# Another order of the first products of the odd projection, and 20 TensorE passes of 256 columns that nothing reads, in the first attention

## The reference

```python
# first block, layer 0: "even" attention (differential and sparse heads), norm, MLP
h = x @ w_in_even
mix = concatenate([diff_attention(...), nsa_attention(...)]) @ w_out_even
x = layer_norm(ALPHA * x + mix)
x = layer_norm(ALPHA * x + square(relu(x @ w_up)) @ w_down)
# layer 1: "odd" attention
h = x @ w_in_odd                      # 1024 x (3 * 1024 + 16)
q, k, v, fl = split(h)                # fl: 16 forget logits a token
mix = forgetting_attention(q, k, v, fl) @ w_out_odd
...
# second block: windowed attention with context, 64 experts of which each token takes 8, final norm
```

## Time and profile before

| | |
|---|---|
| median of 3 runs | 1353.12 us |
| the runs | 1361.75, 1348.17, 1353.12 us |
| the profiled execution's own time | 1348.86 us |
| its span, first to last instruction | 1347.2 us |
| mean granted TensorE clock | 0.998 of 2.4 GHz |
| TensorE busy | 1317.1 us, 98% of the span |

### The profile page before, as it was taken

How to read it: one execution, slowest core, us unless ns; L and a number is a source line. 1 busy time by engine, 2 the same in 40 slices (tenths; PEclk the granted TensorE clock), 3 DMA queues, 4 the chain that set the end, 5 groups by cost and what they waited for, 6 DMA issues and landing times.

```text
span 1347.2 us, 19389 instructions
## 1 busy us (share of the span) xinstructions
PE 1317.1 (98%) x7490; PEld 818.7 (61%) x7490; DVE 679.6 (50%) x1260; ACT 234.1 (17%) x547; POOL 96.1 (7%) x116
## 2 busy tenths in 40 slices
PE   9999999999999999999999999999999999999996
PEld 8676585786679557587686666644444444444433
DVE  1226588877889549977878253421222122212213
ACT  2136211110120341120122252100000000000002
POOL 1116400000011120000000100000000000000001
PEclk9999999999999999999999999999999999999999
DMA  9921155554414535567664504499999999999994
GB/s 379 359 110 66 63 219 206 216 229 191 188 63 169 219 147 217 216 253 285 240 237 158 186 31 190 176 421 422 420 420 414 421 422 420 422 421 422 420 420 196
DMA packets 51008, 359.56 MB, mean 267 GB/s; under 512 B 5888, under 2 KB 6096, under 8 KB 8432
## 3 DMA queue, kind: packets, MB, share of 16 engines
q1 hardware_dynamic: 45248, 324.60, 59.7%
q0 software_dynamic: 5392, 32.05, 6.5%
q10 hardware_dynamic: 288, 1.80, 0.3%
HBM read 356.88 MB, written 1.05 MB: 266 GB/s over the span
## 4 chain that ended last, share of the span: by engine, by line
PE 76%; DVE 11%; DMA 2%; issue 2%; ACT 1%; DVEq 0%; SPq 0%; ACTq 0%
PE ps L1519 13%; PE ps L997 11%; PE ps L988 7%; PE ps L1548 7%; PE ps L1444 7%; PE ps L1497 7%; PE ps L970 5%; PE ps L1274 4%; DVE ring L2358 2%; PE ps L1269 2%; DVE masked_and_probs L2317 2%; DMA ring<-in_stream 2%; PE ps L890 1%; PE ps L909 1%; PE ps L851 1%
## 5 line engine op out<-in xcount | busy, mean ns | idle before, releaser
L2807 DVE TENSOR_TENSOR masked_and_probs<-ps,gate_rows 128x512 f32<-128x512 f32 x52 | 33.5, 686 | 152.4 <-PE ps L1548 152.4
L1497 PE MATMUL ps<-masked_and_probs,probT 128*128 128x512 f32 x208 | 94.4, 594 | 1.0 <-DVE masked_and_probs L2807 1.0
L1444 PE MATMUL ps<-masked_and_probs,mix_rows 128*128 128x256 f32 (+1 forms) x416 | 93.0, 376 | 0.0
L1444 PEld LDWEIGHTS ps<-masked_and_probs,mix_rows 128*128 128x128 f32 x416 | 75.0, 190 | 28.8 <-issue 19.6
L988 PEld LDWEIGHTS ps<-xT,ring 128*128 128x128 f32 x768 | 87.8, 192 | 3.8 <-issue 3.8
L988 PE MATMUL ps<-xT,ring 128*128 128x128 f32 x768 | 88.7, 275 | 0.0
L997 PE MATMUL ps<-ring,qk_tiles 128*128 128x512 f32 x192 | 85.2, 592 | 0.0
L970 PE MATMUL ps<-ring,xT 128*128 128x512 f32 x192 | 83.8, 593 | 0.0
L2795 DVE TENSOR_TENSOR masked_and_probs<-masked_and_probs,ps 128x256 f32<-128x256 f32 x26 | 10.9, 421 | 142.0 <-ACT masked_and_probs L1980 142.0
L1656 ACT ACTIVATE qk_tiles<-ps 128x512 f32<-128x512 f32 (+7 forms) x58 | 30.1, 521 | 244.4 <-PE ps L988 236.7
L1519 PE MATMUL ps<-ring,vec_rows 128*32 128x512 f32 (+2 forms) x296 | 72.0, 592 | 0.0
(11 more groups left out here) (498 smaller groups left out, 2368.1 us busy)
## 6 DMA issues: line engine op xcount, KB each, us to landing
ring<-in_stream SPq DMA_DIRECT2D x200, 1024.0 KB, 10.0
qk_tiles<-in_stream SPq DMA_DIRECT2D x46, 1024.0 KB, 20.3
v_rows<-in_ada POOLq DMA_DIRECT2D x12, 1024.0 KB, 5.2
qk_tiles<-in_ada POOLq DMA_DIRECT2D x12, 1024.0 KB, 5.1
vec_rows<-in_stream SPq DMA_DIRECT2D x12, 1024.0 KB, 17.7
con<-in_stream SPq DMA_DIRECT2D x12, 1024.0 KB, 18.6
y_rows<-in_stream SPq DMA_DIRECT2D x12, 1024.0 KB, 20.3
par<-in_stream SPq DMA_DIRECT2D x12, 1024.0 KB, 20.5
```

The source lines that it names most:

```text
L1444: mm = pe.matmul(ps[:, 5 + kk // 2, kk % 2 * 2 * P:kk % 2 * 2 * P + width], h2[:, t, k * P:(k + 1) * P], select[:, t, 0:width], start=t == ...
L1497: mm = pe.matmul(ps[:, q, :], probT[:, buf, 256 + q // 2 * P:256 + (q // 2 + 1) * P], yslot[:, q % 2 * 512:(q % 2 + 1) * 512], start=False ...
L2807: dve.tensor_tensor(yslot[:, cols], ps[:, 5 + half, :], gaterow[:, 1, cols], ALU.mult).then_inc(ready, 1)
```

## The change

In turns 14 to 33 of the first attention, TensorE does one more matmul of 256 columns (the identity against the cosine table, two passes), just ahead of the turn's transposes and into the bank that they then overwrite. It stands behind the wait for the copy of turn u - 2 and ahead of the wait for the turn's exponential; to allow that, the two waits change places in all turns.

At the start of the odd projection, the forget logits are made in two halves, the first of them directly behind `odd(0, 1)`; the transposes of the second half of the tokens move from ahead of `odd(0, 2)` into its middle; and ScalarE copies product 1 out before it copies the turned half 1.

```diff
+FILLED = {**dict.fromkeys(range(14, 34), 256)}
...
                     if a <= u < b:
                         nk = UNITS[u][3]
+                        if u >= 2:
+                            wait_probs(u - 2)
+                        if u in FILLED:
+                            pe.matmul(ps[:, 2 + u % 2, 0:FILLED[u]], ident, C("cos1")[:, 0:FILLED[u]], start=True, stop=True)
                         pe.wait_ge(s_exp, u + 1)
-                        if u >= 2:
-
-                            wait_probs(u - 2)
...
-            def few_columns(name, width, bank):
+            def few_columns(name, width, bank, cols=slice(0, T)):
...
-                    mm = pe.matmul(ps[lo:lo + 32, bank, 0:T], par[:, at + k * width:at + k * width + 32], xT[:, k, :],
+                    mm = pe.matmul(ps[lo:lo + 32, bank, cols], par[:, at + k * width:at + k * width + 32], xT[:, k, cols],
...
-            def odd(b, n, ks=range(4)):
+            def odd(b, n, ks=range(4), within=None):
...
                     for m in range(4):
+                        if within and m == 2:
+                            within()
...
             odd(0, 1)
-            turn_rows(x, "ln1", 1)
-            odd(0, 2)
+            few_columns("wforget", 16, 4, slice(0, P))
+            odd(0, 2, within=lambda: turn_rows(x, "ln1", 1))
             wait_columns("ln1", 1)
-            few_columns("wforget", 16, 4).then_inc(s_fcol, 1)
+            few_columns("wforget", 16, 4, slice(P, T)).then_inc(s_fcol, 1)
             odd(0, 3)
...
             mlp(0)
-            stds_and_turns("ln1")
+            std(0)
+            take_turn("ln1", xT, only=0)
+            std(1)
+            act.wait_ge(s_prod, odd_product(0, 1))
+            copy(odd_p1, ps[:, ODD_BANKS[0][1], :], scale=SCALE).then_inc(s_taken, 1)
+            take_turn("ln1", xT, only=1)
```

More of the change, by code:

```diff
@@ L902, in attention @@
                         nk = UNITS[u][3]
-                        pe.wait_ge(s_exp, u + 1)
                         if u >= 2:
                             wait_probs(u - 2)
+                        if u in FILLED:
+                            pe.matmul(ps[:, 2 + u % 2, 0:FILLED[u]], ident, C("cos1")[:, 0:FILLED[u]], start=True, stop=True)
+                        pe.wait_ge(s_exp, u + 1)
                         for t in range((nk + P - 1) // P):
@@ L1870, in _ @@
                 scale = SCALE if b == 0 else 1.0
-                act.wait_ge(s_prod, odd_product(b, 1))
-                copy(odd_p1, ps[:, ODD_BANKS[b][1], :], scale=scale).then_inc(s_taken, 1)
-                if b == 0:
+                if b:
+                    act.wait_ge(s_prod, odd_product(b, 1))
+                    copy(odd_p1, ps[:, ODD_BANKS[b][1], :]).then_inc(s_taken, 1)
+                else:
                     act.wait_ge(s_fcol, 1)
```

## The result

| | before | after |
|---|---|---|
| median of 12 runs beside each other | 1351.66 us | 1362.8 us |
| lowest and highest | 1347.38, 1361.75 us | 1351.73, 1368.05 us |
| profiled execution: own time, span | 1348.86, 1347.2 us | 1365.31, 1363.6 us |
| its mean granted clock | 0.998 | 0.985 |

The ratio is 1.0068 [1.0039, 1.0098]: slower, by the medians 11.1 us, by the means 8.6 us (1361.5 for 1352.9). The forecast was 1353.7 us, with a range of 1350 to 1360. Five of the twelve runs lie in that range and two near the forecast (1352.58 and 1355.19 us); six lie at 1365 to 1368 us and draw the median up.

A forecast was written before the change was run, and what follows sets the result against it. TensorE, busy for 98% of the span, was taken to bound the kernel. To the profiled 1348.86 us, 6.1 us for the passes were added and 1.3 us for the new order subtracted: 1353.7 us, range 1350 to 1360.

The forecast's parts named there:

- The price of the passes: First attention, turns 14 to 33: twenty matmuls cost 8.65 us of TensorE, of which 6.1 us are added.
- The hidden part: First attention: 2.3 to 2.7 us of the passes, taken as 2.55, fall where TensorE would have waited anyway.
- that rival (1350.6 us): First attention: VectorE hides most fillers, only those of turns 27 to 33 pay, 3.0 us; chance 0.12.
- The new order: Odd projection's start: product 3 begins 1.3 us earlier, with some 0.5 us of new waiting for VectorE; bounds 0 and 2.1.
- The rival by which it gives nothing: Odd projection: VectorE, moved back 1.2 us, is late for a later product, giving 1355.0 us; chance 0.08.
- The rest moves along: Behind the first attention: TensorE stays busy and loads move with it, so nothing of the shift is absorbed.
- The sum: Whole kernel: profiled execution's 1348.86 us + 6.1 - 1.3 = 1353.7 us; chance 0.5, own range 1352 to 1356.
- the one on the clock: At both edits: granted clock is 1.00, so there is none to give back and unread passes are pure cost.
- the slower draws have another cause and stay: Whole kernel: slow runs remain, so the middle of the runs carries the sum, 1353.12 + 4.8 = 1357.9 us; chance 0.2.
- the first rival: First attention: fillers hold a clock some executions lose, all runs at 1353.7 us; gain over 1% had chance 0.04.
- no idle time of TensorE there is longer than 1.4 us: Windows of both edits: short idle times, given beside the granted clock of 1.00, 2.4 GHz.
- The slower case: First attention's stretch: clock falls despite the passes; slower by over 1% from 13 us at lower level, 1366.7 us; chance 0.05.

The follow-up runs named there:

- c4: The changed kernel plus four 256-column matmuls that nothing reads in the second attention's wait for VectorE; median 1353.07 us, ratio to before 0.998.
- d4: Kernel before plus the 20 passes and four unread matmuls in the second attention's wait, old order of the odd projection; median 1355.26 us, ratio 1.0014.
- f4: Kernel before plus the 20 passes alone, old order of the odd projection, run a second time; median 1360.36 us, ratio 1.0042.
- c1: The control: kernel before with nothing changed, run for the clock of each run; median 1354.54 us, ratio 0.9997.
- d2: Changed kernel without the 20 passes, plus four unread matmuls in the second attention's wait; median 1349.45 us, ratio to before 0.9988.
- e2: Kernel before plus five unread 256-column matmuls in the first MLP's last step, everything behind 2.2 us later; median 1356.35 us, ratio 1.0025.
- e3: Kernel before plus eight unread 256-column matmuls in the first MLP's last step, everything behind 3.5 us later; median 1351.51 us, ratio 1.0001.
- f2: Changed kernel without the 20 passes, plus two unread matmuls in the first MLP's last step, 0.87 us of delay; median 1358.96 us, ratio to before 1.0011.
- c2: Kernel before plus the 20 passes alone, old order of the odd projection; median 1359.99 us, ratio 1.0024.
- d1: The changed kernel unchanged, run again beside the kernel before; median 1360.36 us, ratio to before 1.0071.
- c3: Kernel before plus the new order of the odd projection alone, no added passes; median 1355.48 us, ratio 1.0001.
- e1: Kernel before plus three unread 256-column matmuls in the first MLP's last step, everything behind 1.3 us later; median 1354.04 us, ratio 1.0003.

## Why the prediction was wrong

**The price of the passes: right.** Predicted 6.1 us added; 6.0 in the profile, 5.2 to 6.3 in the runs. The hidden part (2.55 us) was right with it, and VectorE did not hide more: that rival (1350.6 us) fell.

**The new order: right in mechanism and place, somewhat small.** Predicted 1.3 us with VectorE late ahead of product 3 by 0.5; the profile has 1.34 and 0.67. By the medians of c4 and d4 it is 2.2 us, and the split of the order alone gives 2.2 and 2.4. Where the other 0.9 us come from is not shown. The two profiles of c4 and d4 have 1.10 us, so it isn't at the edit; a short fall at the odd projection's start that the old order has in some runs (in f4's profile product 2 takes 5.4 us for the 3.8 of full clock) and the second layer's MLP, whose length varies by as much, are candidates. The rival by which it gives nothing fell.

**The rest moves along: nearly.** "I let nothing be absorbed" held to within 2.2 us: that much came back in the second layer's MLP in the profile of after, and 1.1 us in that of c4_gap_filled (5.35 us behind before at the second attention, 4.2 by the spans).

**The sum: right for the work.** 4.8 us predicted; 4.6 and 5.0 measured by the split, and 4.3 in c4_gap_filled, of which 0.7 are its filler. The forecast's 1353.7 us is within 0.6 us of c4_gap_filled's median, 1353.07, and within 1.3 of it less the filler.

**The step that failed is the one on the clock**: "In this execution there is no clock to give back, and passes that nothing reads are pure cost", and what was built on it: the likeliest case summed onto the profiled execution, near the lower edge of before's own runs, with "The clock reads 1.00 as before" as what the profile after would show. Of the 9.1 us between forecast and median, 2.8 are the base (before's median was 1351.66 us in the comparison, the profiled execution 1348.86) and nearly all the rest, some 6 us, is that after lost the clock more than before did. The term of the clock in the sum was nothing. The spread of before, 1348 to 1362 us, was seen and matched in size with a clock at half speed, but the places looked at were those of the edits. The runs showed three places where the clock falls in some executions: the first attention (profiles of c1, d2, e2, e3, f2), the start of the odd projection in the old order (c2, e2, f4) and, longest, the second attention behind a wait of 1.4 us (after, d1, c2, c3, e1, e2). The change seems to close the first two: in the first attention no profile of 8 with passes lost the clock, for 5 of 10 without; at the odd projection none of 10 with the new order, for 3 of 8 with the old, few enough to be chance. It leaves the third, the dearest: 6 of 13 profiles fall there, none of the 5 in which the wait is filled. Whether after's runs lost more there than before's is not shown, since no run tells where its clock fell; by the mean clock they lost more in all. So the rival "the slower draws have another cause and stay" (0.2, 1357.9 us) came nearest in mechanism, since the middle of the runs carries the sum; it lacked that the draws can also get worse, and its time was 4.9 us short of the median. Of the first rival, that the fillers hold a clock which some executions lose, one half held: they hold it where they stand. Its other half, that all runs then agree at 1353.7 us, needed one filler more, in a place of which the trace had the row: the 1.38 us wait at 461.03 us, as long as the one that the new order removes.

That "no idle time of TensorE there is longer than 1.4 us" was used as a reason for a full clock; just such waits precede the falls in two of the three places.

**The slower case** (the clock falls although the passes are there, from 13 us of work at the lower level, 0.05) happened in size in the profiled execution, but elsewhere: 34.1 us at the lower level cost 14.3 us, within its price of a half for each us spent there, in a stretch it didn't name.

By the Trainium skill's page "TensorE: Matmul & The Clock Gate" (Part 1, HAM oscillation) the clock falls to half after TensorE has waited. The direction was borne out in the second attention. The page's example is a wait on DMA of some 3 to 5 us, longer than any at the three places here, whose longest is 1.47 us (c3_order_only); TensorE was busy for four fifths of the 7 us ahead of the fall, and for nine tenths of the 3.4 us ahead in the control's first attention. The same page has it that transposes don't count as busy like matmuls (Part 4, PE-mode transpose). That would fit the first attention, but no run here isolates it.

## What to carry to other kernels

When the runs of a kernel spread by more than the edit is worth, take the mean clock of each run before anything else, and look for the places where TensorE waits between short matmuls (here 1.4 us in two of them, several times under half a us in the third), in the whole kernel and not only at the edit; one profile with the full clock proves nothing about them. Work that nothing reads, put into such a wait, can cost little and be worth more than the edit: here 3 matmuls in one wait, and 5 instead of 20 in the first attention, took a 0.7% loss to a 0.4% gain. Price the fillers by the number that holds the clock, not by the number of turns.

## What the runs showed of the hardware that was not expected

- The clock fell behind a single wait of 1.38 to 1.47 us of TensorE, with 5.4 to 5.6 us of work in the 7 us ahead, in some executions and not in others of the same program. In the six profiles that show it in the second attention, the fall begins 0.2 to 1.7 us behind the start of the sums that end the wait (465.43 us and 467.1 in after's, 459.64 and 459.9 in c3's).
- Four matmuls of 256 columns that nothing reads, put into that wait, kept the mean clock at 0.997 or more in 12 runs of 12 (c4_gap_filled), for 2 of 24 without them (after, d1_after_again). Three to eight such matmuls elsewhere did not: 17 of 36 runs at 0.992 or less (e1, e2, e3).
- Once down it stayed down for 3.4, 10.2, 13.7, 20.5 or 34.1 us, although TensorE was shown busy for the whole of most of these stretches (20.50 of 20.50 us in c3's).
- A us at the lower level cost less than half a us of the kernel's time: 14.3 us for 34.1, 3.7 for 13.7; over 137 runs 1.05 us for each 0.001 of mean clock.
